# Attention steps of a two-block transformer kernel gathered on fewer marks between half units

## The reference

```
for layer in range(2):                      # first block
    proj = rms_norm(x, g) @ w_in            # queries, keys, values, gates
    o_sb  = stick_breaking(q, k, v)   * silu(gate)    # 6 heads: "sb", three groups of 2 heads
    o_mb  = moba(rotary(q), rotary(k), v) * silu(gate) # 6 heads: "mb", three groups of 2
    o_mem = softmax(q mk) mv          * silu(gate)    # 4 heads: "mem", one group of 4
    x = x + concat(o_sb, o_mb, o_mem) @ w_out
x = rms_norm(x)
# second block: 16 windowed heads with sinks ("swa", four groups of 4),
# 8 differential heads with an rms norm per head ("diff", eight groups of 1),
# gates, two branch projections, w_out, then silu(a) * b @ w_ffn_out
```

## Time and profile before

| | |
|---|---|
| median of 3 runs | 835.77 us (835.47 to 835.83) |
| profiled execution, its own time | 835.07 us |
| span, first to last instruction | 833.2 us |
| mean granted clock of TensorE | 0.991 |
| PE busy | 804.4 us, 97% of the span |
| PEld, DVE, ACT, POOL busy | 653.5, 498.2, 467.9, 136.7 us |
| chain that ended last | 85% PE, of it 68 points on line 1177 |

### The profile page before, as it was taken

The page is one execution under the profiler, slowest core; times in us unless marked ns, Lnnn a source line. Parts: engine busy times, 40 slices in busy tenths (PEclk is TensorE's granted clock), DMA queues, the critical chain, the costliest instruction groups (busy, mean ns, idle before and its releaser), DMA issues.

```text
span 833.2 us, 12690 instructions
## 1 busy us (share of the span) xinstructions
PE 804.4 (97%) x4238; PEld 653.5 (78%) x4238; DVE 498.2 (60%) x731; ACT 467.9 (56%) x1004; POOL 136.7 (16%) x204
## 2 busy tenths in 40 slices
PE   7999999999999997889999999999999999999996
PEld 5877878887777885877778888778887888888885
DVE  5456566584665556646665767666687544555453
ACT  5677585575666565455656565654657433453352
POOL 2011021000342110534433546000000000000000
PEclk9999999999999999989999999999999999999999
DMA  8974553468764636532233444456775645466631
GB/s 249 274 186 144 143 172 102 150 189 267 237 194 129 222 118 195 165 95 78 78 93 96 120 116 167 130 177 227 239 229 165 202 144 185 154 200 195 209 127 51
DMA packets 147295, 137.78 MB, mean 165 GB/s; under 512 B 15025, under 2 KB 115649, under 8 KB 147233
## 3 DMA queue, kind: packets, MB, share of 16 engines
q1 hardware_dynamic: 145136, 129.89, 50.7%
q0 software_dynamic: 2096, 7.09, 3.1%
HBM read 135.90 MB, written 1.05 MB: 164 GB/s over the span
## 4 chain that ended last, share of the span: by engine, by line
PE 85%; POOL 4%; ACT 4%; DVE 3%; issue 2%; DMA 1%; SPq 0%; DVEq 0%; ACTq 0%; POOLq 0%
PE psum L1177 68%; PE psum L1155 7%; PE psum L1276 4%; PE psum L1411 3%; ACT w_hi L1458 1%; POOL rtmp L1123 1%; PE psum L1379 1%; POOL rtmp L1125 1%; PE psum L1197 1%; POOL rtmp L1127 1%; PE psum L1337 1%; POOL stage L1129 1%; ACT probs L1585 1%; DVE w_lo L1654 1%; DMA raw<-in_w_in 1%
## 5 line engine op out<-in xcount | busy, mean ns | idle before, releaser
L1654 DVE TENSOR_TENSOR w_lo<-raw,w_hi 128x1024 fp32r<-128x1024 f32 (+1 forms) x234 | 273.6, 1191 | 121.3 <-ACT w_hi L1458 86.3
L1177 PE MATMUL psum<-w_hi,h_hi 128*128 128x512 f32 (+1 forms) x656 | 260.1, 397 | 4.6 <-DVE h_lo L1712 3.6
L1458 ACT ACTIVATE w_hi<-raw 128x1024 fp32r<-128x1024 f32 (+1 forms) x234 | 230.8, 1011 | 44.3 <-PE psum L1177 18.6
L1177 PE MATMUL psum<-w_lo,h_hi 128*128 128x512 f32 (+1 forms) x656 | 247.6, 377 | 0.0
L1177 PE MATMUL psum<-w_hi,h_lo 128*128 128x512 f32 (+1 forms) x656 | 247.0, 377 | 0.0
L1177 PEld LDWEIGHTS psum<-w_hi,h_hi 128*128 128x128 f32 x656 | 124.6, 190 | 31.2 <-issue 14.6
L1177 PEld LDWEIGHTS psum<-w_lo,h_hi 128*128 128x128 f32 x656 | 124.3, 189 | 19.2
L1177 PEld LDWEIGHTS psum<-w_hi,h_lo 128*128 128x128 f32 x656 | 124.7, 190 | 15.4
L1177 PE MATMUL psum<-w_hi,m_hi 128*128 128x512 f32 x152 | 60.3, 397 | 1.6 <-DVE m_lo L1712 1.5
L1177 PE MATMUL psum<-w_lo,m_hi 128*128 128x512 f32 x152 | 59.3, 390 | 0.0
L1177 PE MATMUL psum<-w_hi,m_lo 128*128 128x512 f32 x152 | 59.2, 389 | 0.0
(11 more groups left out here) (171 smaller groups left out, 1002.6 us busy)
## 6 DMA issues: line engine op xcount, KB each, us to landing
raw<-in_w_in SPq DMA_DIRECT2D x112, 256.0 KB, 3.9
raw<-in_w_ffn_in SPq DMA_DIRECT2D x88, 256.0 KB, 4.1
raw<-in_w_in SPq DMA_DIRECT2D x24, 512.0 KB, 4.0
raw<-in_w_out SPq DMA_DIRECT2D x24, 512.0 KB, 3.7
raw<-in_w_in SPq DMA_DIRECT2D x64, 192.0 KB, 2.7
raw<-in_w_ffn_out SPq DMA_DIRECT2D x22, 512.0 KB, 4.5
meta_w<-in_w_in SPq DMA_DIRECT2D x10, 1024.0 KB, 7.8
raw<-in_w_mem_kv SPq DMA_DIRECT2D x8, 512.0 KB, 3.9
```

The lines of the kernel that those rows point to most:

```text
L1177: last = nc.tensor.matmul(psum[:, bank, 0:n], sx[name][:, c, t * P:(t + 1) * P], wx[:, kk, 0:n], start=u["first"] and kk == 0 and z == 0, ...
L1458: nc.scalar.activation(weights(u)[0][:, :, 0:n], raw[:, u["raw"], :, 0:n], ACT.Copy)\
L1654: nc.vector.tensor_tensor(lo[:, :, 0:n], raw[:, u["raw"], :, 0:n], hi[:, :, 0:n].bitcast(F32), ALU.subtract)\
```

## The change

Only the table of marks is changed. The steps themselves, their instructions and their buffers stay.

```diff
-    "sb": dict(turn_qk=(1,), gate=(1.25, 2.25), scores=(3, 3), later=(4, 4.5), out=(7.75, 7.5),
-               turn_mix=(9,)),
-    "mb": dict(turn_qk=(2.5,), gate=(2.25, 4.25), scores=(3, 3), soft=(3.5, 3.5), turn_p=(4.5, 5), out=(5.5, 7),
-               turn_mix=(7.5,)),
+    "sb": dict(turn_qk=(0.75,), gate=(1.25, 2.25), scores=(3, 3), later=(4.5, 4.5), out=(7.5, 7.5),
+               turn_mix=(8.5,)),
+    "mb": dict(turn_mix=(6.5,), turn_qk=(2.5,), gate=(2.25, 4.25), scores=(3, 3), soft=(3.5, 3.5), turn_p=(4.5, 4.5),
+               out=(5.5, 5.5)),
     "mem": dict(turn_qk=(1,), gate=(0.25, 2.25), scores=(1.75, 1.75, 4.25, 4.25), soft=(2.25, 2.25, 4.75, 4.75),
-                turn_p=(4, 5.25, 6.5, 7.5),
-                out=(5.75, 6.75, 7.75, 8.75), turn_mix=(9.75,)),
-    "swa": dict(turn_qk=(3.25, 2.75), scores=(4.45, 4.45, 6.45, 6.45), soft=(4.95, 4.95, 6.95, 6.95),
+                turn_p=(4, 4, 6, 6),
+                out=(5.25, 5.25, 7, 7), turn_mix=(8,)),
+    "swa": dict(turn_qk=(3, 3), scores=(4.45, 4.45, 6.45, 6.45), soft=(4.95, 4.95, 6.95, 6.95),
...
-    "diff": dict(turn_qk=(1.5, 2.5), scores=(4.25, 4.25), soft=(4.75, 4.75), blend=(6.25,), turn_p=(7.75,), out=(8.75,),
-                 turn_mix=(9.75,)),
+    "diff": dict(turn_qk=(1.5, 3), scores=(4.25, 4.25), soft=(4.75, 4.75), blend=(6.25,), turn_p=(7.75,), out=(9.5,),
+                 turn_mix=(10.75,)),
```

## The result

The changed kernel takes 842.86 us (median of 6 executions, 840.22 to 847.75) beside 835.23 us for the kernel before: ratio 1.0101, 95% interval 1.0078 to 1.0124. Run again later it took 840.10 us beside 833.51 us, ratio 1.0088 (1.0069 to 1.0106). It is slower, as forecast, but by 6.6 to 7.6 us where 2.7 were forecast, and 842.9 lies 1.1 us above the range.

The account below looks back on a forecast made before the run. TensorE, busy 97% of the span, was taken to bound the kernel, with its waits. Waits and switches sum to +1.05 us, one clock drop adds 1.6: +2.7 us, 837.8 profiled, 838.5 us as median; range 833.6 to 841.8.

Parts of the forecast that it names:

- memory norm and place A: Layer 0: sb 1's paired value products wait for m_lo, +1.4 us; `turn_mix` of sb 0 leaving the norm's mark, -0.4 us.
- place B: Layer 0, sb 2's outputs and mb 0's probabilities: three ring users at one mark, second `turn_p` waits 1.7 us; cost 0.95 us.
- place C: Layer 0, mem and mb 1: `turn_p` waits on banks held by mem's `turn_mix` and the last `turn_norm`; cost 0.95 us.
- place D, with the waits that go in layer 1: Layer 1: waits of 0.8 us go, but mb 0's second `turn_p` waits about 1.7 us behind mem's `turn_mix`; cost 0.9 us.
- swa: Query-turn waits for POOL stay; one mark at its end holds three ring users instead of four, gain 0.25 us.
- diff and gates: Differential heads: 1.0 us gained on query-turn waits for POOL, 0.5 on `turn_p` waits; 0.3 at the gates' first half unit.
- 31 fewer switches: Marks with PE work fall from 182 to 151; at 0.01 to 0.04 us per switch, a gain taken as 0.7 us.
- lower clock: One drop from 2.4 to 1.2 GHz, behind the layer 0 value-product wait of about 1.9 us printed; +1.6 us.
- The second rival: Clock falls at two to four of the places with long waits; median 840.0 to 843.2 us; chance 0.19.
- The two rivals that ended at or below the kernel before: One or both slow swa stretches go, 833.6 us, chance 0.16; marks do nothing as ACT and DVE have slack, 835.1 to 835.8, 0.08.

Follow-up runs that it names:

- diff alone: Kernel before with only the new marks of diff (`out` 9.5, `turn_mix` 10.75, second query turn 3): 833.99 us beside 833.88, ratio 1.0008.
- the pair with transposes: Kernel before plus 144 unread transposes in gates 1 to 3: one behind each matmul, 850.28 us; six together per half unit, 851.80 us.
- The two orders of `turn_mix`: Kernel before with new diff marks: `turn_mix` behind the blend (10.75), 833.99 us; ahead of it (10.2, second query turn at 2.5), 832.55 us.

## Why the prediction was wrong in size

The direction was right, and so were the four places; the time was not. By its own terms, in us ("measured" is by row in the second trace of the changed kernel, clean, where nothing else is said):

| term | forecast | measured |
|---|---|---|
| memory norm and place A | +1.0 | +1.5 |
| place B | +0.95 | +1.15 |
| place C | +0.95 | +1.24 |
| place D, with the waits that go in layer 1 | +0.9 | +0.95 |
| swa | -0.25 | +0.2 (from 392 us on, beyond what diff alone costs there) |
| diff and gates | -1.8 | +0.3 (diff alone) |
| 31 fewer switches | -0.7 | -0.05 (0.002 each, from the pair with transposes) |
| sum | +1.05 | +6.2 (by the clean time of 12 executions) |
| lower clock | +1.6 | +1.8 (mean of 12 executions) |

The measured terms add up to 5.3. Another 0.6 us stands between 295 and 392 us, around the last norm and swa 0, in this trace and in that of the new marks of sb, mb and mem (0.1 us in the first trace of the changed kernel). Part of it is the reckoning: in the kernel before, 0.6 us of the wait at 368.03 us lie in a stretch at the lower clock that is taken out whole. The rest is open.

**diff is the step that failed, by 2.1 us.** The mechanism was right as far as it went: POOL's series got shorter (by 1.44 us in the changed kernel, 0.57 us in diff alone), as forecast from the two durations of the same operation, and the waits for it went. What the sum left out stood in its own brackets, as a bound: `turn_mix`, now behind the blend on DVE, holds its bank. I took the two waits of `turn_p` as a gain of 0.5 us and did not walk DVE's new order for one head. It is blend (to 498.9), split, then m_lo at 499.68, against a `turn_p` due at 499.8. Walking it would have given the 0.37 us at those heads. The gates were the other part: 0.3 us of gain was forecast for the wait at their first half unit, and that wait went, but the later `turn_mix` of the last head made a longer one at the second group, 0.45 us lost in all. The two orders of `turn_mix` show its place as the cause of both: +0.3 us behind the blend, -1.64 us ahead of it. The second query turn moved half a unit with it, and its share alone was not run, but the wait that went was one for m_lo.

**The switches were sized from the wrong view.** The pitches of the earlier trace rows are uneven around any small work, but the same unevenness is there once for each group of matmuls, and the 0.01 to 0.04 us were read off rounded starts. The two runs give 0.002 us, for a switch to transposes of 128 columns and back; other small work was not tried.

**The places were mis-sized on one side.** A, B and C came out 0.2 to 0.5 us above their terms. B's lacked the gate product of DVE. Just before the memory norm a `turn_mix` of sb 0 now waits for o_st (0.28 us printed), which ate the gain of 0.4 us there (the wait of 0.39 us fell to 0.16 us printed); the prediction had only the gain. Each term had been taken in the middle of its bounds, and every surprise was one more wait.

**The clock term was right on average by luck.** One fall was forecast, behind A. Over the 12 executions the loss is 1.1 stretches more than before, with an error of about as much, and it is not one fall behind A in each: 7 of the 12 lost no more than the kernel before does on average, and the profiled one had four stretches more than the profiled one of before. The second trace has falls behind both A and B, and yet a clock of 0.993, since it shows none near 12 us, at the last norm, and at swa's second wait, where the trace of before has one each. The second rival named several falls and gave 840.0 to 843.2 us, which holds both medians, but its 3.2 to 6.4 us of clock are not the reason for it: 6.2 of the 8 us are waits. The upper end of the range, 841.8, was said to be three drops, which add up to 841.6.

The prediction took the Trainium skill ("TensorE: Matmul & The Clock Gate", section "A second HAM failure mode: psum-queue depth-cycling") to mean that all four places would drop; the section itself tells of frequent short idling and of no single wait. The traces agree with that reading at A and B (6 of 7), hardly at C (1 of 5) and not at D (0 of 4).

The two rivals that ended at or below the kernel before both fell: swa's slow stretches stayed in the changed kernel (363.05 us waits 1.89, 379.02 us 1.88), and 40% idle on ACT and DVE did not keep the read-outs early.

## What to carry to other kernels

Work that shares a small ring of buffers is not to be counted by what it saves in switches, but by who holds the buffer two places back, and how late that holder's reader comes in its own engine's queue. Before steps are put together, write out the order of every engine for one period. When a wait is moved off one engine, that order tells what is late next; here the same four steps of a head cost 0.3 us in one order and gave 1.6 us in the other. And look first at the longest waits of the kernel before: taking two of them away in swa, and the order in diff, gave 4 us, while the 31 marks gave nothing.

## What the runs showed of the hardware

A long wait of TensorE is followed by the lower clock only in some executions, even of the same program: C's 1.75 us in the first trace of the changed kernel and not in the second. These are waits, start to start, of the twelve traces without added transposes (those of the first 16 us are left out), and how many had a stretch at 0.50 beginning during them or up to 2 us behind:

| wait | us | lower clock |
|---|---|---|
| place A, new marks | 2.16 | 3 of 4 |
| place B, new marks | 2.17 | 3 of 3 |
| swa 0, query turn | 1.90 to 2.11 | 9 of 10 |
| swa 0, first `turn_p` | 2.04 to 2.36 | 7 of 11 |
| last norm of layer 1, for a DMA of `meta_w` | 2.10 to 2.42 | 4 of 12 |
| place C, new marks | 1.75 | 1 of 5 |
| place D, new marks | 1.85 | 0 of 4 |
| last projection, `m_lo` | 1.64 | 0 of 12 |
| same norm, third wait, for h_lo | 0.9 to 1.4 | 5 of 12 |
| place C, old marks | 1.36 | 0 of 7 |

The two rows of the last norm are these waits, 5 us apart, here in the kernel before:

```profile
327.77 1.91 PE L1197 MATMUL psum<-meta_w,meta_s 128*16 128x512 f32 x16 [2.17 <-DMA meta_w<-in_w_in]
...
332.86 0.41 PE L1177 MATMUL psum<-w_hi,h_hi 128*128 128x384 f32 x1 [1.25 <-DVE h_lo L1712]
```

They break an order by length: the longest waits of the table are followed by a fall in 4 of 12, and waits of at most 1.4 us that follow others closely in 5 of 12. So length alone does not decide, and what else does is open; A's wait of 2.16 us was followed by either level. The falls also bring most of the scatter of the time: over the 12 executions of the changed kernel the clean time spans 2.5 us, and what the lower clock takes 9.4 us.

Lone transposes of 128 columns between matmuls of 512 columns cost TensorE hardly more than six in a row, 0.11 us each.
